# Dense layers entered by depth tile with a weight part rounded ahead, a down-projection moved ahead of gathered rows, and four weight rests on GpSimd

## The reference

```python
def sqrelu_mlp(hn, w1, w2):
    return jnp.square(jax.nn.relu(hn @ w1)) @ w2          # 1024 -> 4096 -> 1024
...
    for layer in range(DEPTH):
        ...                                               # mixer: recurrence (0), attention (1)
        h = h + g1[:, None, :] * y
        hn = modulate(rms_norm(h, norm2_g[layer]), sh2, sc2)   # rms_norm(h) * (1 + sc2) + sh2
        h = h + g2[:, None, :] * sqrelu_mlp(hn, mlp_w1[layer], mlp_w2[layer])
...
    for e in range(N_EXPERTS):                            # mixture of experts, first model
        he = jax.nn.silu(t @ w_gate[e]) * (t @ w_up[e])
        y = y + combine[:, e:e + 1] * (he @ w_down[e]).astype(jnp.float32)
```

## Time and profile before

| | us |
|---|---|
| median of 3 runs (1903.07 to 1905.93) | 1904.51 |
| profiled execution | 1903.74 |
| span of that execution, first to last instruction | 1902.1 |
| TensorE busy in it (matmuls) | 1827.5 |
| VectorE busy | 759.7 |
| ScalarE busy | 661.9 |
| GpSimd busy | 65.4 |
| mean granted clock of TensorE, share of 2.4 GHz | 0.991 |

### The profile page before, as it was taken

One profiled execution on the slowest core, in us unless ns is written; L12 is line 12 of the kernel. 1 busy time (PEld: TensorE's weight loads), 2 busy tenths in 40 slices (PEclk: granted clock), 3 DMA queues, 4 the chain that ended last, 5 costly groups with the idle time before them and its releaser, 6 DMA issues.

```text
span 1902.1 us, 28392 instructions
## 1 busy us (share of the span) xinstructions
PE 1827.5 (96%) x11833; PEld 1292.6 (68%) x11850; DVE 759.7 (40%) x1278; ACT 661.9 (35%) x1064; POOL 65.4 (3%) x128
## 2 busy tenths in 40 slices
PE   5999999989999999999999999999999999899998
PEld 3888785323335888784333336766699989679998
DVE  4593553000004683652000004213355567656554
ACT  2325441111114325532111122141255556645443
POOL 0000001100001000001100010000000000000000
PEclk9999999999999999999999999999999999999999
DMA  9769955999976675865999956879955433444440
GB/s 379 305 266 388 351 243 237 429 428 426 428 300 271 250 288 225 316 265 238 427 426 428 413 200 280 352 311 419 396 205 201 177 133 116 152 153 177 177 176 22
DMA packets 52753, 540.87 MB, mean 284 GB/s; under 512 B 6768, under 2 KB 11248, under 8 KB 21680
## 3 DMA queue, kind: packets, MB, share of 16 engines
q1 hardware_dynamic: 42800, 505.66, 65.9%
q0 software_dynamic: 9856, 33.82, 4.7%
HBM read 589.53 MB, written 28.84 MB: 325 GB/s over the span
## 4 chain that ended last, share of the span: by engine, by line
PE 81%; DMA 9%; DVE 6%; DVEq 1%; ACT 1%; issue 1%; SPq 0%; POOL 0%; POOLq 0%; ACTq 0%
PE bank L1358 14%; PE bank L991 11%; PE bank L993 11%; PE bank L992 10%; PE bank L1383 6%; PE bank L1028 6%; DMA ring<-in_w_up 5%; PE bank L1037 4%; PE bank L1561 3%; PE bank L1161 2%; PE bank L1488 1%; PE bank L1509 1%; DMA ring<-in_lru_w_out 1%; PE bank L981 1%; PE bank L1336 1%
## 5 line engine op out<-in xcount | busy, mean ns | idle before, releaser
L991 PE MATMUL bank<-split_x,split_w 128*128 128x256 f32 x1024 | 285.5, 279 | 2.3 <-DVE split_w L2780 2.3
L992 PE MATMUL bank<-split_x,split_w 128*128 128x256 f32 x1024 | 286.8, 280 | 0.0
L993 PE MATMUL bank<-split_x,split_w 128*128 128x256 f32 x1024 | 286.3, 280 | 0.0
L2662 DVE TENSOR_TENSOR hidden<-cqkv,bank 128x256 f32<-128x256 f32 x46 | 19.4, 421 | 514.9 <-ACT cqkv L1913 514.9
L991 PEld LDWEIGHTS bank<-split_x,split_w 128*128 128x128 f32 x1024 | 192.5, 188 | 3.3 <-DVE split_w L2780 3.3
L993 PEld LDWEIGHTS bank<-split_x,split_w 128*128 128x128 f32 x1024 | 192.5, 188 | 0.0
L992 PEld LDWEIGHTS bank<-split_x,split_w 128*128 128x128 f32 x1024 | 192.3, 188 | 0.0
L2780 DVE TENSOR_TENSOR split_w<-ring,split_w 128x1024 fp32r<-128x1024 f32 x128 | 156.3, 1225 | 89.0 <-ACT split_w L2048 89.0
L992 PE MATMUL bank<-hx_lo,ring_lo 128*128 128x256 f32 (+1 forms) x656 | 183.4, 280 | 0.0
L2048 ACT ACTIVATE split_w<-ring 128x1024 fp32r<-128x1024 f32 x128 | 134.2, 1053 | 88.1 <-PE bank L993 87.4
L991 PE MATMUL bank<-hx_hi,ring_lo 128*128 128x256 f32 (+1 forms) x528 | 150.3, 285 | 0.0
(11 more groups left out here) (402 smaller groups left out, 2833.8 us busy)
## 6 DMA issues: line engine op xcount, KB each, us to landing
ring<-in_ada SPq DMA_DIRECT2D x48, 2048.0 KB, 11.6
ring<-in_w_gate SPq DMA_DIRECT2D x32, 2048.0 KB, 13.3
ring<-in_w_up SPq DMA_DIRECT2D x32, 2048.0 KB, 18.4
ring<-in_w_down SPq DMA_DIRECT2D x32, 2048.0 KB, 16.8
ring<-in_mlp_w SPq DMA_DIRECT2D x32, 2048.0 KB, 7.6
ring<-in_w_in SPq DMA_DIRECT2D x16, 2048.0 KB, 11.6
mix<-in_w_gate SPq DMA_DIRECT2D x14, 2048.0 KB, 15.7
mix<-in_w_up SPq DMA_DIRECT2D x14, 2048.0 KB, 20.2
```

The source lines that it names most:

```text
L991: pe.matmul(out, hi, x_hi, start=start, stop=False, **kw)
L992: pe.matmul(out, hi, x_lo, start=False, stop=False, **kw)
L993: return pe.matmul(out, lo, x_hi, start=False, stop=stop, **kw)
```

## The change

It has four parts.

1. **Entry of the dense layers.** The eight depth tiles are handled one by one. VectorE computes tile times gain times scale in one instruction (`scaled_stream`, eight of 128x256); ScalarE adds the shift as a bias while it rounds (`round_stream`, eight of 128x256); VectorE makes the remainder from tile, shift and rounded value in one instruction (`stream_lo`, eight, after all eight of the first). ScalarE rounds weight part 0 of the first turn behind its last square and ahead of its wait for the norm's sum (`before_mlp_act`), and VectorE writes that part's rest ahead of its wait for the scale (`before_mlp_dve`). TensorE's drain moves ahead of the sum of squares, its filling matmuls shrink from 14 and 20 to 6 and 4, and part 0 runs in the order hi products by half of the depth, then products with the activation's remainders by half (`column_part_by_halves`). The three loops are written so that the roundings of the next turn's parts 0 to 3 stand at the end of a turn; the last two turns are written out.
2. **Experts.** The last block's transposes stand between the second and the third quarter of the previous block's down-projection, and its own down-projection ahead of both groups of gathered rows. ScalarE's copy of those transposes moves ahead of its weighting of the first gathered rows.
3. **Attention.** The rests of parts 24 to 27 are written by GpSimd, after its expert work, each behind ScalarE's rounding; TensorE waits for GpSimd's step instead of VectorE's.
4. The lists of named steps follow.

```diff
@@ moe_steps: order of TensorE's and ScalarE's steps
+        last = [f"hT{n}"] * (n == NB - 1)
+        pe += [f"hT{n - 1}"] * (n > 0) + [f"gu{n}"] + pair + last + [f"d{n - 1}"] * (n > 0)
@@ TensorE, experts
                     for k in range(4):
+                        if n == NB - 2 and k == 2:
+                            hidden_rows(NB - 1)
                         for g in range(2):
...
-                hidden_rows(NB - 1)
-                earlier_results(0)
                 down(NB - 1)
-                earlier_results(1)
+                for t in range(TT):
+                    earlier_results(t)
@@ TensorE, first part of a dense turn
+        def column_part_by_halves(pe, j, out, hi_ready, lo_ready):
+            for k in range(KT):
+                if k % 4 == 0:
+                    hi_ready(k // 4)
+                pe.matmul(out, part_hi(j)[:, k, :], h_hi[:, k, :], start=(k == 0), stop=False)
+                pe.matmul(out, part_lo(j)[:, k, :], h_hi[:, k, :], start=False, stop=False)
+            for k in range(KT):
+                if k % 4 == 0:
+                    lo_ready(k // 4)
+                ins = pe.matmul(out, part_hi(j)[:, k, :], h_lo[:, k, :], start=False, stop=(k == KT - 1))
+            return ins
@@ TensorE, entry
+            before_mlp_pe(0)
             sum_squares(r_job("norm2"), h_t, KT, AR, SQ2).then_inc(PR.sem, PR.one("norm2"))
...
-                pe.drain().then_inc(pe_steps.sem, pe_steps.first)
-                keep_busy(pe, banks[4 if layer else 7], 14)
-                pe.wait_ge(h2.sem, h2.at(H2[0]))
+                keep_busy(pe, banks[4 if layer else 7], 6)
+                pe.wait_ge(lo.sem, lo.at(H2_SCALED[0]))
                 clear_sums(pe)
-                keep_busy(pe, banks[4 if layer else 7], 20)
-                pe.wait_ge(h2.sem, h2.at("h lo1"))
+                keep_busy(pe, banks[4 if layer else 7], 4)
@@ GpSimd, behind its expert work
+            for n in range(24, 28):
+                pool.wait_ge(AA.sem, AA.at(f"part{n}"))
+                nc.gpsimd.tensor_tensor(a_part(n, ring_lo), a_part(n, ring), as_f32(a_hi(n)), ALU.subtract)\
+                    .then_inc(GA.sem, GA.one(f"part{n}"))
@@ ScalarE, entry
-            def round_stream(A, V, turn=0):
-                for i in range(2):
-                    act.wait_ge(V.sem, V.at(H2[i], turn))
-                    half = slice(4 * i, 4 * i + 4)
-                    act.activation(h_hi[:, half, :], h_t[:, half, :], ACT.Copy).then_inc(A.sem, A.one(f"h hi{i}"))
+            def round_stream(A, V):
+                for k in range(KT):
+                    act.wait_ge(V.sem, V.at(H2_SCALED[k]))
+                    act.activation(h_hi[:, k, :], h_t[:, k, :], ACT.Identity, bias=mod[:, 3 * KT + k:3 * KT + k + 1])\
+                        .then_inc(A.sem, A.one(H2_HI[k]))
...
+                if meanwhile:
+                    meanwhile()
                 act.wait_ge(Pj.sem, Pj.at(name))
                 rstd(act, bank[name], rs[:, 0, :], D).then_inc(A.sem, A.one(name))
...
+            def mlp_round(layer, base, it, pair, j):
+                ...
+                if j % 4 == 0:
+                    s = slots[j // 4]
+                    act.wait_ge(ring_full[s], it * 16 + 16 * (base[s] + 1))
+                act.activation(part_hi(j), mlp_raw(slots, j), ACT.Copy)\
+                    .then_inc(act_steps_.sem, act_steps_.one(f"hi{j}"))
+            def before_mlp_act(layer, base):
+                act.drain().then_inc(MLP[layer][1].sem, MLP[layer][1].first)
+                mlp_round(layer, base, 0, 0, 0)
...
+            norm_act(AR, VR, PR, r_bank, SQ2, "norm2", [VR.at(f"out{i}") for i in range(4)],
+                     lambda: before_mlp_act(0, M0_BASE))
...
+            before_mlp_act(1, M1_BASE)
             act.wait_ge(PA.sem, PA.at("norm2"))
@@ VectorE, entry
+            def scaled_stream(V):
+                for k in range(KT):
+                    stt(h_t[:, k, :], x_t[:, k, :], amod[:, KT + k:KT + k + 1], rs[:, 0, :], ALU.mult, ALU.mult)\
+                        .then_inc(V.sem, V.one(H2_SCALED[k]))
+            def stream_lo(V, A):
+                for k in range(KT):
+                    dve.wait_ge(A.sem, A.at(H2_HI[k]))
+                    ins = stt(h_lo[:, k, :], h_t[:, k, :], mod[:, 3 * KT + k:3 * KT + k + 1], as_f32(h_hi[:, k, :]),
+                              ALU.add, ALU.subtract)
+                    if k % 4 == 3:
+                        ins.then_inc(V.sem, V.one(f"h lo{k // 4}"))
...
+            before_mlp_dve(0)
             dve.wait_ge(AR.sem, AR.at("norm2"))
-            modulated(x_t, amod[:, KT:2 * KT], mod[:, 3 * KT:4 * KT], rs[:, 0, :], VR, H2)
+            scaled_stream(VR)
             stream_lo(VR, AR)
@@ VectorE, attention
-            rest_of_a_parts(24, 28)
```

More of the change, by code:

```diff
@@ L124 @@
 H2 = ["h2 0", "h2 1"]
+H2_SCALED = [f"h2 scaled{k}" for k in range(8)]
+H2_HI = [f"h2 hi{k}" for k in range(8)]
 SQ0 = [f"sq0 {i}" for i in range(4)]
@@ L1951, in _ @@
                     if n == NB - 1:
+                        hidden_rows(n)
                         weighted_rows(0)
@@ L2028, in _ @@
             act.activation(cqkv[:, 0:512], banks[7][:, :], ACT.Copy).then_inc(AR.sem, AR.one("mod rows"))
-            norm_act(AR, VR, PR, r_bank, SQ2, "norm2", [VR.at(f"out{i}") for i in range(4)])
-            round_stream(AR, VR)
+            def mlp_round(layer, base, it, pair, j):
+                pe_steps, act_steps_, _ = MLP[layer]
+                e = it * 2 + pair
+                slots = MLP_SLOTS[layer][2 * pair:2 * pair + 2]
+                act.wait_ge(pe_steps.sem, pe_steps.at(f"part{(j + 4) % 8}", e - 1 if j < 4 else e))
+                if j % 4 == 0:
[3 more added lines that the diff above has]
+                    .then_inc(act_steps_.sem, act_steps_.one(f"hi{j}"))
@@ new lines, in turn @@
+                def turn(it, pair, last=False):
+                    e = it * 2 + pair
+                    for m in range(4):
+                        act.wait_ge(pe_steps.sem, pe_steps.at(f"part{m}", e))
+                        act.activation(sg[:, m, :], banks[MLP_BANK[m]][:, 0:T], ACT.Relu)
+                        act.drain()
+                        act.activation(he[:, m, :], sg[:, m, :], ACT.Square)\
+                            .then_inc(act_steps_.sem, act_steps_.one(f"g{m}"))
+                        mlp_round(layer, base, it, pair, m + 4)
+                    if not last:
+                        for j in range(4):
+                            mlp_round(layer, base, it + pair, 1 - pair, j)
@@ new lines, in mlp_act @@
+                for j in range(1, 4):
+                    mlp_round(layer, base, 0, 0, j)
+                with act.Fori(0, MLP_TURNS // 2 - 1) as it:
+                    for pair in range(2):
+                        turn(it, pair)
+                for pair in range(2):
+                    turn(MLP_TURNS // 2 - 1, pair, pair == 1)
+            norm_act(AR, VR, PR, r_bank, SQ2, "norm2", [VR.at(f"out{i}") for i in range(4)],
+                     lambda: before_mlp_act(0, M0_BASE))
+            round_stream(AR, VR)
@@ L2764, in _, with mlp_rest, before_mlp_dve @@
             into_x(VR, PR, r_bank, mod[:, 2 * KT:3 * KT])
+            def mlp_rest(layer, it, pair, j):
+                _, act_steps_, dve_steps_ = MLP[layer]
+                slots = MLP_SLOTS[layer][2 * pair:2 * pair + 2]
+                dve.wait_ge(act_steps_.sem, act_steps_.at(f"hi{j}", it * 2 + pair))
+                tt(part_lo(j), mlp_raw(slots, j), as_f32(part_hi(j)), ALU.subtract)\
+                    .then_inc(dve_steps_.sem, dve_steps_.one(f"lo{j}"))
+            def before_mlp_dve(layer):
+                dve.drain().then_inc(MLP[layer][2].sem, MLP[layer][2].first)
+                mlp_rest(layer, 0, 0, 0)
+            before_mlp_dve(0)
             dve.wait_ge(AR.sem, AR.at("norm2"))
-            modulated(x_t, amod[:, KT:2 * KT], mod[:, 3 * KT:4 * KT], rs[:, 0, :], VR, H2)
+            scaled_stream(VR)
             stream_lo(VR, AR)
```

112 lines of the change are left out of this document (48 added, 64 removed).

## The result

| | before | after |
|---|---|---|
| median of the runs (4 of each) | 1903.93 (1903.07 to 1905.93) | 1888.08 (1886.8 to 1888.93) |
| profiled execution | 1903.74 | 1888.35 |
| its span | 1902.1 | 1886.8 |
| mean granted clock | 0.991 | 0.992 |

The ratio is 0.9919, with a 95% interval of 0.9907 to 0.9932: the changed kernel is faster by 0.8%, 15.4 us between the profiled executions. (Before has a fourth run here, 1903.36, beside the three of its own table.) The forecast was 1891 with a range of 1887.5 to 1896. One run further on, 3653.44 us of the kernel with the experts part alone, was a slow one and stands in no median or ratio here.

The account below looks back on a forecast made before the run. TensorE, holding 81% of the chain, was taken as the bound, so edits pay only where it stands, runs slowly or waits on serial work. Gains 2.2 + 3.8 - 2.0 + 5.3 + 3.6 = 12.9 from 1903.74 gave 1891 us; range 1887.5 to 1896.

Parts of the forecast that it names:

- Expert layers: Ends of both expert layers: gains of 2.2 and 3.8 us, the latter 2.1 stall plus 1.7 slow transposes.
- A dense entry by itself: Dense-layer start: part 1 8.1 us after scaling begins, not 12.05, gaining 3.9; in attention's layer 3.6, after 0.3 late.
- The rival of a falling clock: Dense entries: gaps between part 0's four pieces lower TensorE's clock, giving 1894 us; chance 12%.
- The recurrent entry: Recurrent layer's dense start: norm waits behind a rounding whose load lands late; loss 1.7 us, put at 2.0.
- the further 0.3 that I added for the clock: Recurrent layer's dense entry: TensorE returns from standing idle at the lower clock, so loss put at 2.0, not 1.7.
- Attention: Before the scores: VectorE, freed of four weight rests, starts on the first score earlier; gain 5.3 us, bounds 3.2 and 5.3.
- the rival with a chance of 20%: Attention: GpSimd's writes overlap VectorE's normalisations on SBUF, costing the overlap, at most 4.6 us; 1893, at most 1896; 20%.
- the 7.4 at which it would have been late: Attention: GpSimd's four writes, if above 7.4 us each, delay the out-projection; slower kernel from 10.6 us each; chance 3%.

Follow-up runs that it names:

- the kernel with the experts part alone: The kernel before with only the expert-layer edits (part 2 of the change); median of six runs 1895.1 us, ratio 0.9961.
- the run with GpSimd's writes held apart: The changed kernel with GpSimd's four writes spaced out, each behind a different group of ScalarE's exponentials; 1893.7 us, ratio 0.9959.
- the mended kernel: The changed kernel with norm ahead of weight part 0, 16 more zero matmuls before it, and one of GpSimd's four writes given to VectorE; 1882.1 us, ratio 0.9895.
- the run with part 3 alone: The kernel before with only the attention edit, GpSimd writing the rests of parts 24 to 27; 1898.0 us, ratio 0.9971.

## Why the prediction came out as it did

- **Expert layers.** Right, in mechanism and size: 2.4 and 4.0 for 2.2 and 3.8. The clock did not fall in layer 1 once the idle time was gone; that was 1.7 of the 3.8.
- **A dense entry by itself.** Right in its steps, low by 0.8. The scalings start 28.99 us behind the out-projection's start and the old multiplication at 28.81, so 0.2 late where I allowed 0.3. From there part 1 takes 7.6 us, where I had 8.1: eight three-operand instructions take 3.25 us in a row, one every 0.396, and I had taken 0.43, with 0.41 as the lower bound. The old entry took 12.16 from there and not 12.05. Together 4.4 instead of 3.6. What the single pieces of the entry give was read from the rows; no run separates them. The rival of a falling clock did not come here.
- **The recurrent entry.** The mechanism stands: the norm waited for a load that landed 24.1 us after its issue, and VectorE's scalings came 5.2 us later than with the norm first. They began 26.4 us behind the issue, as forecast; the 7.6 instead of 8.1 behind them make the loss 1.2 where the steps gave 1.7, and the further 0.3 that I added for the clock was not due: it fell, but was back at 1.00 from 1368, before nearly all of part 0. The place of the fall varies: in the trace of the run with GpSimd's writes held apart it reached part 0 and cost 0.3. I costed TensorE's moved drain at nothing. That held only because the wait for the load covered it; in the mended kernel it costs 0.4 us.
- **Attention.** The step that failed is that GpSimd's writes end without meeting VectorE. The start of the scores did gain 5.2 us, and the rival with a chance of 20% took 1.46 of it back, which leaves the 3.8 of the run with part 3 alone; the table's 4.1 has the 0.4 of VectorE's pause on top, which came with part 1. The rival's mechanism was told rightly, its price as an overlap of up to 2 us; its time of 1893 did not come, since other terms were larger. Its bound, at most the 4.6 us taken from VectorE, is wrong: with the writes 10 us later 8.2 were lost. And GpSimd's write took 2.36 us, far from the 7.4 at which it would have been late.
- **What no step of the sum contained.** 2.4 us of the router and -0.8 at the start, both of which differ between executions of one kernel (the start by up to 2.1 us in three traces of the changed one). Without these the profiled execution would have been near 1889.9, against the 1890.8 of my sum. Yet the medians of all three measurements lie at 1888 where the kernel before has 1904, so some 2 us are gained that no step of the sum explains and no run traced. The 0.8 in between are -1.2 in attention's start, +0.8 in each of the entries and +0.4 in the experts: errors of both signs that nearly cancel, which is luck.

## What to carry to other kernels

A piece of work moved ahead "because the engine is idle there" brings its waits along: look up when its input lands, and if that is later than the wait it was put in front of, put it behind. Before handing VectorE's work to GpSimd, list which instructions of VectorE will run beside it and keep the short ones that follow each other away from it; one write moved back was worth 1.5 us. And split a comparison into stretches between instructions that both traces share, with a repeat of one of the kernels: a sum that comes out right can hide a term of each sign.

## What the runs showed of the hardware that I had not expected

*One instruction for one.* Four short instructions of VectorE on SBUF beside four writes of GpSimd took 9.10 us instead of 0.88, each held to the end of a write, while VectorE's other forms beside the four writes of after kept their length: reading scores from PSUM 0.68 us, reducing from SBUF 0.69, a reciprocal 0.17. SBUF — State Buffer of the Trainium skill (§ SBUF: two separate sides) says that the loser of the shared ports waits for the winner's whole instruction; the traces agree, and add that a queue of several is paid once per instruction of VectorE. The write itself took 2.36 us in after, near the 2.3 estimated from GPSIMD Engine Reference of the Trainium skill (§3.1).

*Two speeds at one granted clock.* Busy time over 80 us in the two dense loops, of two executions of the changed kernel; the first loop, then the second, for each:

```profile
1397.00:1477.00 80.00, 80.00 (x688) 80.00 (x687) 46.41 (x61) 41.80 (x61) 0.00 (x0) 1.00 0.50 186
...
1720.00:1800.00 80.00, 80.00 (x682) 80.00 (x681) 43.64 (x54) 39.35 (x56) 0.00 (x0) 1.00 0.51 191
```

```profile
1397.00:1477.00 80.00, 80.00 (x681) 80.00 (x680) 46.04 (x61) 41.45 (x60) 0.00 (x0) 1.00 0.50 185
...
1720.00:1800.00 80.00, 80.00 (x688) 80.00 (x687) 44.40 (x55) 39.14 (x56) 0.00 (x0) 1.00 0.51 191
```

TensorE is full and the clock is 1.00 in all four, yet it does 688 matmuls in one and 681 or 682 in the other, and each execution has the slow loop in another place. The last loop took 176.6 or 178.3 us in the traces of this case, nothing between. That is 1.7 us of scatter which no edit explains; what sets it is open.
